# Head pairs with the values as weights, two attention steps in flight, and modulation vectors on four column groups

## The reference

```
def _modulation(cvec, w_mod, b_mod):
    m = jax.nn.silu(cvec) @ w_mod + b_mod
    return jnp.split(m[:, None, :], 6, axis=-1)

def _attend(q, k, v):                       # 8 heads, q and k of 64+32, v of 64
    s = jnp.einsum("bqhd,bkhd->bhqk", q, k) * ATT_SCALE
    p = jax.nn.softmax(s, axis=-1)
    return jnp.einsum("bhqk,bkhd->bqhd", p, v)

# per layer: m_x = _modulation(c, ...), m_c = _modulation(c_ctx, ...)
# h = rmsnorm(x)*(1+scale)+shift; mix = (g_a*att@w_oa + g_b*fourier@w_ob + g_c*pool@w_oc)@w_out
# x = x + gate*mix;  x = x + gate*peer(h2)   (peer: 128 gathered rows a token of two tables)
```

## Time and profile before

| | us |
|---|---|
| median of 3 runs | 4782.97 (4778.31 to 4784.37) |
| the profiled execution | 4788.78 |
| its span in the profile | 4787.0 |
| TensorE busy | 3656.0 (76%) |
| VectorE busy | 2585.5 (54%) |
| POOL busy | 1985.9 (41%) |
| ScalarE busy | 811.1 (17%) |
| bytes moved | 1328 MB, mean 277 GB/s |

### The profile page before, as it was taken

How to read it: one execution, slowest core, us unless ns; L and a number is a source line. 1 busy time by engine, 2 the same in 40 slices (tenths; PEclk the granted TensorE clock), 3 DMA queues, 4 the chain that set the end, 5 groups by cost and what they waited for, 6 DMA issues and landing times.

```text
span 4787.0 us, 34613 instructions
## 1 busy us (share of the span) xinstructions
PE 3656.0 (76%) x10558; PEld 1808.0 (38%) x10558; DVE 2585.5 (54%) x5494; ACT 811.1 (17%) x1937; POOL 1985.9 (41%) x2088
## 2 busy tenths in 40 slices
PE   7779487888677789877786875777768895676776
PEld 3258343455343224532244321221356663322111
DVE  1211568455788534676225784576453333677676
ACT  1110112211111112211111111111132111111111
POOL 0000266555566444566103674566000000576775
PEclk9879799999879999976897998755868997899756
DMA  4223599999999998999637999999200003899999
GB/s 172 88 100 128 206 353 336 352 364 382 353 381 359 352 380 301 387 399 365 210 129 281 366 397 364 347 405 374 78 1 1 1 1 134 321 401 362 408 407 353
DMA packets 389102, 1328.11 MB, mean 277 GB/s; under 512 B 38604, under 2 KB 43980, under 8 KB 385336
## 3 DMA queue, kind: packets, MB, share of 16 engines
q0 software_dynamic: 301824, 1099.07, 60.4%
q1 hardware_dynamic: 80944, 204.09, 11.6%
q10 hardware_dynamic: 6152, 22.74, 1.3%
HBM read 1324.58 MB, written 1.17 MB: 277 GB/s over the span
## 4 chain that ended last, share of the span: by engine, by line
PE 27%; DMA 19%; DVE 7%; POOL 6%; issue 5%; ACT 2%; ACTq 0%; DVEq 0%; SPq 0%; POOLq 0%
PE ps L1449 26%; DMA arena<-in_peer_up,arena 9%; POOL arena L2661 5%; DMA arena<-in_peer_v,arena 4%; DVE arena L721 3%; DVE arena L734 2%; DMA arena<-in_w_mod 2%; ACT arena L2125 2%; DMA arena<-in_peer_down,arena 2%; DMA arena<-in_peer_u,arena 1%; PE ps L1455 1%; DMA arena<-mod_scratch 1%; ACT L2125 0%; DMA arena<-in_ada_w 0%; DMA arena<-in_w_out 0%
## 5 line engine op out<-in xcount | busy, mean ns | idle before, releaser
L1449 PE MATMUL ps<-arena 128*128 128x512 f32 (+10 forms) x9820 | 3534.5, 510 | 897.0 <-DMA arena<-in_peer_up,arena 338.2
L1449 PEld LDWEIGHTS ps<-arena 128*128 128x128 f32 (+4 forms) x9820 | 1704.8, 198 | 2670.5 <-issue 1536.3
L734 DVE SCALAR_TENSOR_TENSOR arena<-arena,ps 128x1024 f32<-128x1024 f32 x1024 | 1240.7, 1216 | 501.8 <-DMA arena<-in_peer_down,arena 325.5
L2661 POOL DMA_INDIRECT arena<-in_peer_down,arena x768 | 739.5, 963 | 1218.7 <-DVE arena L738 654.8
L2661 POOL DMA_INDIRECT arena<-in_peer_up,arena x768 | 735.7, 958 | 484.9 <-PE ps L1449 318.3
L2125 ACT ACTIVATE arena<-arena 128x128 f32<-128x128 f32 (+5 forms) x1250 | 447.6, 385 | 2159.5 <-PE ps L1449 959.9
L2661 POOL DMA_INDIRECT arena<-in_peer_u,arena x256 | 243.1, 950 | 815.5 <-DVE arena L738 722.7
L734 DVE SCALAR_TENSOR_TENSOR ps<-arena,ps 128x512 f32<-128x512 f32 x508 | 382.9, 754 | 139.5 <-DMA arena<-in_peer_up,arena 105.6
L721 DVE TENSOR_TENSOR arena<-ps,arena 128x512 f32<-128x512 f32 (+3 forms) x198 | 135.5, 684 | 583.2 <-PE ps L1449 560.3
L2125 ACT ACTIVATE arena<-ps 128x512 f32<-128x512 f32 (+3 forms) x345 | 175.2, 508 | 1094.0 <-PE ps L1449 746.1
L1455 PE MATMUL ps<-arena 128*128 128x128 f32 (+2 forms) x738 | 146.3, 341 | 228.0 <-DVE arena L721 158.9
(11 more groups left out here) (33 smaller groups left out, 501.5 us busy)
## 6 DMA issues: line engine op xcount, KB each, us to landing
arena<-in_w_mod SPq DMA_DIRECT2D x24, 2048.0 KB, 15.2
arena<-in_gate_blocks SPq DMA_DIRECT2D x16, 2048.0 KB, 10.6
arena<-in_w_in SPq DMA_DIRECT2D x14, 2048.0 KB, 16.7
arena<-in_w_pq SPq DMA_DIRECT2D x12, 2048.0 KB, 10.1
arena<-in_ada_w POOLq DMA_DIRECT2D x24, 1024.0 KB, 5.6
arena<-in_w_out SPq DMA_DIRECT2D x8, 2048.0 KB, 13.3
arena<-in_gate_blocks SPq DMA_DIRECT2D x8, 1792.0 KB, 9.9
arena<-mod_scratch ACTq DMA_DIRECT2D x26, 512.0 KB, 8.3
```

Source lines behind the costliest of these rows:

```text
L734: self.e.scalar_tensor_tensor(o, a, s, b, op0, op1, accum_out=accum).then_inc(*(inc or self.inc(self.S.vec)))
L1449: return self.e.matmul(o, l, r, start=start, stop=stop)
L2661: self.e.indirect_dma_start(out=o, out_offset=None, in_=table, in_offset=bass.IndirectOffsetOnAxis(ap=idx.bitcast(U32), axis=0)).then_inc( ...
```

## The change

Attention (`attend`, all engines): the steps run over s = 2h + t, so both query tiles of a head follow each other. Scores of s stand ahead of the transposes of s-2. The transposed probabilities of a head are gathered for both tiles in `PT` (4 x 256), and for each pair of heads the values (128 x 64) are the weights and the probabilities (256 columns) move: head 0 writes output partitions 0-63, head 1 64-127, alternately, which gives `AT` without a transpose of the result. The row sums of all 16 steps are inverted at the end, spread over columns, transposed and multiplied onto `AT`. The copies of the transposed probabilities stay shared (VectorE even steps, ScalarE odd ones). Units: 38 instead of 82; in the context attention they cost 0.97 instead of 0.45.

Modulation: the eight products of a vector go to four groups of 32 output partitions, by k modulo 4, as four partial sums (weights of 32 columns, of which the first 2 or 1 count). ScalarE copies the bank out, and a product with a constant 128 x 3 table (`quad`) sums the partial rows into a second bank. `modvec` has two units a vector, `modhalf` three, without the slices. Vectors 4 to 11 of layer 0 come by `modhalf` (halves on POOL's queue, rate 0.4) instead of `modvec` (SP's queue, rate 0.13). Biases get two buffers each. In `x_second` the rate is 0.65 instead of 0.55, and the rings are split 5 and 3 banks instead of 6 and 2.

The diff, cut to its core:

```
-GROUP0 = ("zeros", "ident", "iota")
+GROUP0 = ("zeros", "ident", "iota", "quad")     # quad = i % 32 == (0, 1, 2)
-         "most": [0, 1, 2, 3, 4, 5], "few": [6, 7]}
+         "most": [0, 1, 2, 3, 4, 5], "five": [0, 1, 2, 3, 4], "few": [5, 6, 7]}
...
-            yield from self.at(0.45, self.attend(2, ...))
+            yield from self.at(0.97, self.attend(2, ...))
-            yield from self.at(3.5, self.modvec(1, T0, range(12)))
+            yield from self.at(1.75, self.modvec(1, T0, range(12)))
-        self.weave(start1(), self.modvec(0, NB - 2048, range(4, 12)), 0.13, slots=("two", "third"))
+        self.weave(start1(), self.modhalf(NB - 2048, [(0, j) for j in range(4, 12)]), 0.4, rings=("five", "few"), slots=("two", "third"))
-        self.weave(x_second(), self.modhalf(K.H2R, vectors), 0.55, rings=("most", "few"), slots=("two", "third"))
+        self.weave(x_second(), self.modhalf(K.H2R, vectors), 0.65, rings=("five", "few"), slots=("two", "third"))
...
 # Tensor
+    def quarters(self, b, w, ks, fresh):
+        for k in ks:
+            g = k % 4
+            i = self.mm(b.ap[32 * g:32 * g + 32, :], self.K.svb[:, 3 * k:3 * k + 32], w[:, k - ks[0], :], fresh and k < 4, k > 3)
+        return i
+    def total(self, l, b, parts):
+        m, c0 = (2, 0) if l < 2 else (1, 2)
+        c = self.bank()
+        self.wait_ge(*self.drained(b))
+        self.wait_ge(*self.vacant(c))
+        self.mm(c.ap[0:m, :], self.K.quad[:, c0:c0 + m], parts, True, True).then_inc(*self.fill(c))
+        return c
     def modvec(self, l, at, js):
...
-            for k in range(8):
-                i = self.mm(b.ap[0:m, :], K.svb[:, k, c0:c0 + m], w[:, k, :], k == 0, k == 7)
+            self.quarters(b, w, range(8), True).then_inc(*self.fill(b))
             self.mark(("w", s.i, s.n))
             yield
+            self.rows_of[j] = self.total(l, b, K.arena[:, at + 1024 + 512 * (j % 2):at + 1536 + 512 * (j % 2)])
+            yield
     def modhalf(self, at, vectors):
...
-                for k in range(4):
-                    i = self.mm(b.ap[0:1, :], K.svb[:, 4 * half + k, c:c + 1], w[:, k, :], ...)
-                    if k == 1:
-                        yield
+                i = self.quarters(b, w, range(4 * half, 4 * half + 4), True)
                 i.then_inc(*(self.fill(b) if half else self.inc(S.half_read)))
                 self.mark(("sums", self.halves_in))
                 yield
+                if half == 0:
+                    if last:
+                        self.total(l, last, parts)
+                    yield
+            last = b
 # Tensor.attend, one step
+        for s in range(19):
+            if s < 16:
+                h, t = s // 2, s % 2
+                b = made[s] = self.bank(first)
+                self.wait_ge(*self.vacant(b))
+                for i, (KT, _) in enumerate(kvs):
+                    ins = self.mm(b.ap[:, 256 * i:256 * i + 256], QT[0:96, h, 128 * t:128 * t + 128], KT[0:96, h, :], True, True)
+                ins.then_inc(*self.fill(b))
+                yield
+            if s % 4 == 2 and s > 2:
...
+                self.wait_ge(*self.drained(was))
+                self.wait_ge(*self.drained(bt))
+                for i in range(nk):
+                    for e in range(2):
+                        h = 2 * p + e
+                        ins = self.mm(ab.ap[64 * e:64 * e + 64, 256 * (p % 2):256 * (p % 2) + 256], kvs[i // 2][1][:, i % 2, 64 * h:64 * h + 64],
+                                      PT[e][:, i, :], i == 0, i == nk - 1)
...
+            if 2 <= s < 18:
...
+                self.wait_ge(*self.drained(made[s - 2]))
+                self.wait_ge(*self.vacant(bt))
+                self.turn4(bt, [(bt.ap[:, 128 * i:128 * i + 128], PB[(s - 2) % 3][:, 128 * i:128 * i + 128]) for i in range(nk)])
+                yield
 # Scalar.attend, one step
+            if 2 <= s < 18:
+                bt = self.bank(second)
+                if s % 2 == 1:
+                    self.evict(bt, PT[(s - 2) // 2 % 2][:, 0:nk, 128:256], ...)
+            if s < 16:
+                h, t = s // 2, s % 2
+                self.wait_ge(*self.next(S.row_max))
+                self.act(PB[s % 3][:, 0:128 * nk], held.ap[:, 0:128 * nk], ACT.Exp, scale=ATT_SCALE, ...)
 # Scalar.modvec: the copy of the partial sums, in the unit of the products
+            b = self.bank()
...
+            self.evict(b, parts, b.ap)
+            yield
```

More of the change, by code:

```diff
@@ L944, in values @@
-        def values(t, h):
-            b = self.bank(inner)
-            yield
-            if h % 2 == 0:
-                self.wait_ge(*self.full(b))
-                self.copy(PT[h % 2][:, 0:128 * nk], b.ap[:, 0:128 * nk], inc=self.drain(b))
-            yield
-        for t in range(2):
-            ab = self.bank(out)
-            for h in range(9):
-                if h < 8:
-                    bs = yield from scores(t, h)
-                if h > 0:
-                    yield from values(t, h - 1)
-            self.wait_ge(*self.full(ab))
-            self.wait_ge(*self.drained(bs))
-            self.recip(rs, rs)
-            self.tt(heads(at), heads(ab.ap), eight(rs), M, inc=self.drain(ab))
-            b = self.bank(inner)
+        rs, nm, mx = K.small[:, 16:32], K.small[:, 32:36], K.small[:, 36:40]
@@ L964, in attend @@
+        self.wait_ge(*self.drained(b))
+        self.wait_ge(*self.full(bt))
+        self.recip(rs, rs)
+        for t in range(2):
+            self.copy(heads(PB[t]), eight(rs[:, 8 * t:8 * t + 8]), inc=self.inc(S.shares))
+        self.wait_ge(*self.drained(ab))
+        for t in range(2):
+            b = self.bank(first)
+            self.wait_ge(*self.full(b))
+            at = AT[:, :, 128 * t:128 * t + 128]
+            self.tt(at, at, units4(b.ap), M, inc=self.drain(b))
             yield
@@ L1484, in modhalf @@
         K, S = self.K, self.S
-        for n, (l, j) in enumerate(vectors):
-            c = 0 if l < 2 else 2
+        parts = K.arena[:, at + 1536:at + 2048]
+        last = None
+        for l, j in vectors:
             b = self.bank()
@@ L1644, in attend @@
-        for t in range(2):
-            ab = self.bank(out)
-            self.wait_ge(*self.vacant(ab))
-            was = None
-            for h in range(9):
-                if h < 8:
-                    bs = yield from scores(t, h)
-                if h > 0:
-                    yield from values(t, h - 1, was, ab)
-                was = bs
-            self.wait_ge(*self.drained(ab))
-            b = self.bank(inner)
-            self.wait_ge(*self.vacant(b))
-            self.turn4(b, [(b.ap[:, 128 * i:128 * i + 128], at[:, 128 * i:128 * i + 128]) for i in range(4)])
+        PT, PB = bufs
@@ new lines, in attend @@
+        first, second, out = self.attend_rings()
+        made = {}
+        for s in range(19):
+            if s < 16:
[5 more added lines that the diff above has]
+                ins.then_inc(*self.fill(b))
+                yield
+            if s % 4 == 2 and s > 2:
+                p = (s - 6) // 4
+                if p % 2 == 0:
+                    ab = self.bank(out)
+                    self.wait_ge(*self.vacant(ab))
+                self.wait_ge(*self.drained(was))
[5 more added lines that the diff above has]
+                                      PT[e][:, i, :], i == 0, i == nk - 1)
+                if p % 2 == 1:
+                    ins.then_inc(*self.fill(ab))
+                yield
+            if 2 <= s < 18:
+                was = bt if s > 2 else None
+                bt = self.bank(second)
+                self.wait_ge(*self.drained(made[s - 2]))
+                self.wait_ge(*self.vacant(bt))
+                self.turn4(bt, [(bt.ap[:, 128 * i:128 * i + 128], PB[(s - 2) % 3][:, 128 * i:128 * i + 128]) for i in range(nk)])
+                yield
@@ L1658, in attend @@
+        for t in range(2):
+            b = self.bank(first)
+            self.wait_ge(*self.next(self.S.shares))
+            self.wait_ge(*self.vacant(b))
+            self.turn4(b, [(b.ap[:, 128 * i:128 * i + 128], PB[t][:, 128 * i:128 * i + 128]) for i in range(4)])
             yield
@@ L2197, in modhalf @@
         K, S = self.K, self.S
+        m = 2 if vectors[0][0] < 2 else 1
+        parts = K.arena[:, at + 1536:at + 2048]
+        for i in range(2):
+            if self.put.get(S.mod_out[i].name, 0):
+                self.wait_ge(S.mod_out[i], self.put[S.mod_out[i].name])
         def store(n, b):
@@ L2670, in fetch @@
             self.wait_ge(*self.K.marks["w", s.i, s.n - 1])
+        if s.i == 2 and self.halves_in:
+            self.wait_ge(*self.K.marks["sums", self.halves_in])
         if s.i == 2 and self.base:
@@ L2697, in modvec, with modhalf @@
             yield
+            yield
+    def modhalf(self, at, vectors):
+        self.halves_in += 2 * len(vectors)
+        yield from self.units_of(3 * len(vectors) + 2)
     def tok_major(self, l, c0, n, dst, HTs):
```

195 lines of the change are left out of this document (94 added, 101 removed).

## The result

The changed kernel takes 4606.38 us (median of 4, 4598.3 to 4613.11) beside 4782.2 for the kernel before: ratio 0.9633 [0.9615, 0.965] (in brackets the 95% interval), 176 us less, where 120 were forecast. It is faster than the whole predicted range. The profiled execution took 4609.44 us, its span 4607.6, 179.4 less than the span before.

What follows compares the result with a forecast made beforehand. Bound by stage: DMA in the gathers, TensorE or its waits and slow clock in the attention stages. Terms -62 - 8 - 6 - 3 - 41 + 0 = -120 us gave 4663 us, own range 4635 to 4700 (4620 to 4745 at 0.80).

Steps and rivals of the forecast that it cites:

- First attention: First attention stage, 137.7 us before: 55.5 us of TensorE at clock 0.85 plus 10 for tail and waits, 75; -62 (-75 to -25).
- One vector: Each modulation vector: products on four groups 2.3 us, summing 0.86, drains 0.5; 3.7 us (serial 8.3) against 7.0.
- program order: Rival: matmul starts and ends keep program order, a vector's products 4.3 us, a vector 5.7; total 4709, chance 0.15.
- no overlap: Rival: column groups do not overlap at all, a vector 8.3 us, attention 43.5; total 4767, chance 0.07.
- 75 to 196.6 us: Stretch ahead of the first attention: 3.4 vectors at 3.7, 12.6 us, against 21.6 before; -8 (-12 to +7 if serial).
- Start: 0 to 75 us: four vectors, each a chain, saving 1.5 us each; -6 (-13 to +6, serial).
- Second attention: Layer-1 attention with the second block's vectors: 67 us of work, 74 at 0.9 clock, 10 idle; 84 against 130, -46.
- Mixing: After the first attention: the first 17 us of the mixing run at a warmer clock, -3 (0 to -4).
- Gathers: Gather stages with context attention and layer-1 vectors: DMA and TensorE both limit, one stays; 0 (-10 to +10).
- slower: Rival: ScalarE's wait stops loads overlapping for layer-1 vectors in the gather, +18.9 us each; total 4890, chance 0.05.
- all better: Rival: a quarter instead of a third for four groups, waits hidden, full clock; -155, total 4628, chance 0.13.
- The clock: Rival: bursts keep TensorE at 1.2 GHz, first attention 115 us; total 4779, no change, chance 0.08.

## Why the prediction was wrong

The sign, the four places and the overlap of the column groups were right; sizes were off, nearly all to the same side, the largest of them the clock and the idle time that I took over from the old attention; and what had slowed that attention I had put down to the wrong wait. By the prediction's own steps:

*First attention, -87.1 against -62; the steps that failed are the clock and the allowance of 10 us for tail and waits.* I had 55.5 us of TensorE work, a clock of 0.85 and 10 us idle: 75. It came to 45.8 busy at a clock of 1.00 and 3.5 idle: 49.3. So -9.7 by the work, -9.8 by the clock, -6.5 by the idle time. The work itself: the attention's shapes add up to 35.0 us (forecast 36.6), a vector to 3.1 (3.7), with 4.5 vectors for 5.1; and the groups' busy times overlap at their ends, which a sum of rows doesn't see. The clock of 0.85 came from a stage whose TensorE stopped at each head. I took it for a property of the mixture of vectors and heads. It held for the old attention beside the new vectors (0.84), but with the product moved the same matmuls ran at 0.89; the new attention had 0.94 with the old vectors and 0.91 without any. So the clock went with how the attention is laid out more than with the vectors beside it. What sets it isn't shown beyond that: the rows don't order by the share of idle time (0.94 with 14.7 of 86.6 us idle, 0.89 with 7.3 of 66.4).

*Which wait hid the gain.* I credited two steps in flight with hiding the maximum and the exponential. One step hides them nearly as well (50.5 us). The wait that cost most in the old attention beside the new vectors was that for the copy of the transposes, right ahead of each product (14.3 of 18.7 us of idle time); it had no term of its own in my sum, and came in only through the clock and the 10 us that I took over.

*One vector, 3.1 against 3.7.* I took a third for the four groups, 2.3 us; from start to start it is the quarter that was my lower bound: in the layer-1 vectors' stretch four waves of four records begin at 1501.77, 1502.22, 1502.65 and 1503.08 us, 0.43 to 0.45 us apart, 1.75 in all. The drains of 0.5 us are there: in the kernel with all vectors ahead of the attention a full-width record begins at 109.08 us and others like it stand 0.35 us apart, but the piece behind it begins at 109.52; its second wave begins at 109.98 and the next full-width record at 110.52, not 0.43 but 0.54 us later. That is some 0.1 us a change, six a vector. 1.75 + 0.9 + 0.5 makes the 3.1 of the rows, so the mis-sized term is the third. The rule of the Trainium skill, "TensorE: Matmul & The Clock Gate", section "Part 3: Packing small matmuls", that gave 2.9 us by its 2.38 times for three groups would have been further off. The rival *program order* (4.3 us of products) is out by the common starts, and so is *no overlap*: one group alone took 7.7 us a vector (34.5 / 4.5) and lost 121 us of the gain.

*75 to 196.6 us, -20.0 against -8.* The vectors were right: 8.9 + 3.3 us for 3.5 of them, forecast 12.6. What was missing lies in the chain of queries and keys. Its rows before, for the two of the changed kernel above:

```profile
L1455 PE MATMUL ps<-arena 128*96 128x128 f32 x48 | 10.8, 400 | 5.4 <-DVE arena L721 3.1 <-DVE arena L738 2.0
L1455 PE MATMUL ps<-arena 128*128 128x128 f32 x8 | 2.7, 386 | 13.2 <-DVE arena L727 13.2
```

TensorE's idle time behind VectorE fell from 18.6 to 13.3 us, and these transposes from 13.5 to 10.6. That the small pieces did it is likely: with whole loads 7 to 9 of the 12 us came back, in one profile.

*Start, -13.2 against -6.* I took 1.5 us a vector, expecting a slow clock to eat most of it. That slowness is in the first chain (waves of four 0.85 us apart, against 0.43 above), but the chain still shortened by 2.6 us (7.57 to 5.0): its products took 3.2 us where I had 4.6, the sum and the hand-overs 1.8 where I had 2.7. Four such make 10, and the third and fourth loads were issued 3.4 and 6.6 us earlier (28.31 and 38.61 us, for 31.66 and 45.19).

*Second attention, -60.8 against -46, and w_oa +3.5 against +5.* I had 67 us of work at a clock of 0.9, 74, and 10 idle. It was busy for 60.4 at 0.98, and idle for the same 10: 70 where 84 stood. The fear that halves arrive late came true in part, 8.5 us of waiting for ada_w.

*Mixing, nothing against -3.* The warmer clock came (1.00 for 0.89 in the first 17 us), but the end of the last vector now lies there, and the stream of products behind the first groups begins 6.1 us into the stage where it began at 6.2.

*Gathers, 0 as forecast.* The rival *slower* (18.9 us more for each layer-1 vector) didn't come: 156.9 us for 154.3. The matmuls of that stretch say why a cheaper vector brings nothing there. Before, 1597 to 1751.5 us:

```profile
L1449 PE MATMUL ps<-arena 128*2 128x512 f32 x176 | 79.1, 601 | 21.1 <-DMA arena<-in_w_mod 21.1
L1449 PE MATMUL ps<-arena 128*128 128x512 f32 x121 | 55.4, 603 | 1.0 <-ACT arena L2125 1.0
```

After, 1475.6 to 1632.5 us:

```profile
L1456 PE MATMUL ps<-arena 128*128 128x512 f32 x121 | 64.0, 662 | 11.2 <-DMA arena<-in_peer_up,arena 11.2
L1456 PE MATMUL ps<-arena 128*32 128x512 f32 x176 | 30.3, 820 | 45.2 <-DMA arena<-in_w_mod 45.2
L1456 PE MATMUL ps<-arena 128*2 128x512 f32 x20 | 10.2, 592 | 0.0
```

30 us of matmul time went (134.5 to 104.5, the sums' 10.2 among it), and the waits for loads and gathers grew from 21 to 56 us. TensorE was not a second limit there, as I had written; the kernel with these vectors elsewhere agrees with the bytes alone (71.7 us for 70).

Of the rivals *all better* (4628) came nearest and still stood 22 us too high: 12 of these in the first attention, where even at full clock it had some 52 us of work and 10 for the tail, against 45.8 and 3.5, and 8 ahead of it. *The clock* (4779) is out by the rows at 0.91 and 1.00.

## What to carry over

When a stage's TensorE is both stopped often and slow, don't carry the clock of the stage before over to the stage after the change: here one removed stop paid 11.4 us as idle time and 8.4 more as faster records. Before restructuring a chain, ask which wait stands directly ahead of a matmul whose input was only just issued; moving that matmul one step later gave half of what the new attention gives in its first stage. In a stretch like the gather here, with a DMA share of 0.95 and more, don't make the compute cheaper, take the bytes out: 25 MB moved to a stage with idle DMA engines gave back 72 us for 42 in the profiles, and about 17 in the medians.

## What the runs showed of the hardware

Four float32 products with 32 weight columns each, on four groups of output partitions, ran at the same time: 72 records of 512 columns took 9.6 us, on one group 34.5, a ratio of 3.6. Two groups of 64 columns overlapped fully where they alternated and in part in blocks of eight: 64 records of 256 columns took 7.8 and 11.5 us, and in blocks the second group began with the fifth record of the first. A change between these shapes of weights and the full width cost some 0.1 us each (0.44 instead of 0.35 us ahead of a piece, 0.54 instead of 0.43 behind it).

The granted clock beside the busy time, from rows above: the same attention and vectors had 0.84 with 67.5 of 86.2 us busy, 0.89 with 59.1 of 66.4, and the new form 1.00 with 45.8 of 49.3; with the old vectors the new attention had 0.94 with 71.9 of 86.6; the old attention alone had 0.50 with 37.3 of 48.3, the new one alone 0.91 with 33.6 of 39.7.
